# ScalarE's Silu of the z gates issued one projection step earlier in a Mamba-2 scan

## The reference

```python
zxbcdt = h @ w_in
z, xbc, dt = jnp.split(zxbcdt, ...)
xbc = jax.nn.silu(causal_depthwise_conv(xbc, conv_w, conv_b))
...                      # xs, bmat, cmat from xbc
y = ssd_chunked_scan(xs, dt, a, bmat, cmat) + d_skip * xs
y = rms_norm(y * jax.nn.silu(z), norm_w)
return y @ w_out
```

## Time and profile before

| | |
|---|---|
| median of 3 runs | 1496.96 us (1496.11 to 1497.39) |
| the profiled execution, its own time | 1497.73 us |
| its span | 1495.9 us |
| granted TensorE clock, mean | 0.991 |
| TensorE (matmul) busy | 1437.1 us, 96% |
| weight loads busy | 976.6 us, 65% |
| VectorE busy | 995.1 us, 67% |
| ScalarE busy | 747.6 us, 50% |
| DMA | 506.01 MB, mean 338 GB/s |

### The profile page before, as it was taken

One profiled execution on the slowest core, in us unless ns is written; L12 is line 12 of the kernel. 1 busy time (PEld: TensorE's weight loads), 2 busy tenths in 40 slices (PEclk: granted clock), 3 DMA queues, 4 the chain that ended last, 5 costly groups with the idle time before them and its releaser, 6 DMA issues.

```text
span 1495.9 us, 18527 instructions
## 1 busy us (share of the span) xinstructions
PE 1437.1 (96%) x6840; PEld 976.6 (65%) x6840; DVE 995.1 (67%) x1271; ACT 747.6 (50%) x977; POOL 18.6 (1%) x27
## 2 busy tenths in 40 slices
PE   7989999999999899999999999999999989999998
PEld 2835787888789778674666556756465655565573
DVE  2578788888659899764666646765654555655563
ACT  3565544444455896353446445644453444545361
POOL 0000000000000000000100000000000000000000
PEclk9999999999999999999999999999999999999999
DMA  9878698888366545679999999999999999999996
GB/s 361 330 248 292 240 396 303 301 295 301 103 217 185 162 161 204 261 288 409 364 412 406 411 374 416 418 420 420 409 420 413 420 420 418 413 420 414 420 419 247
DMA packets 118201, 506.01 MB, mean 338 GB/s; under 512 B 13779, under 2 KB 16492, under 8 KB 83032
## 3 DMA queue, kind: packets, MB, share of 16 engines
q1 hardware_dynamic: 115640, 496.51, 85.6%
q0 software_dynamic: 2464, 8.24, 1.6%
HBM read 502.52 MB, written 2.32 MB: 337 GB/s over the span
## 4 chain that ended last, share of the span: by engine, by line
PE 74%; DVE 10%; DMA 7%; ACT 6%; issue 3%; SPq 0%; DVEq 0%; ACTq 0%
PE acc L2685 16%; PE acc L2693 16%; PE acc L2686 16%; PE acc L3187 15%; DVE w_lo L1581 3%; ACT w_hi L1038 2%; DVE cv L2308 2%; DMA raw_rest<-in_moe_w_down 1%; DMA raw<-in_moe_w_down 1%; PE xb L3071 1%; DMA mod<-in_moe_w_gu 1%; PE acc L2834 1%; DMA mod<-in_moe_w_down 1%; DMA raw<-in_ada_w 1%; ACT dec L1487 1%
## 5 line engine op out<-in xcount | busy, mean ns | idle before, releaser
L1581 DVE TENSOR_TENSOR w_lo<-raw,w_hi 128x1024 fp32r<-128x1024 f32 x356 | 427.3, 1221 | 136.6 <-ACT w_hi L1038 126.1
L1038 ACT ACTIVATE w_hi<-raw 128x1024 fp32r<-128x1024 f32 x356 | 371.0, 1057 | 249.1 <-PE acc L2693 157.7
L2685 PE MATMUL acc<-w_hi,g_hi 128*128 128x512 f32 x448 | 179.3, 400 | 4.0 <-ACT w_hi L1038 3.9
L2686 PE MATMUL acc<-w_hi,g_lo 128*128 128x512 f32 x448 | 174.8, 390 | 0.0
L2685 PE MATMUL acc<-w_hi,a_hi 128*128 128x512 f32 x384 | 155.4, 405 | 8.5 <-ACT z_s L1404 7.7
L2686 PE MATMUL acc<-w_hi,a_lo 128*128 128x512 f32 x384 | 151.4, 394 | 0.0
L2693 PE MATMUL acc<-w_lo,g_hi 128*128 128x512 f32 x448 | 139.1, 392 | 4.1 <-DVE w_lo L1581 4.1
L3187 PE MATMUL acc<-raw,g_s 128*64 128x512 f32 x592 | 131.6, 594 | 0.5 <-DMA raw<-in_moe_w_gu 0.5
L2693 PE MATMUL acc<-w_lo,a_hi 128*128 128x512 f32 x384 | 119.5, 392 | 0.0
L1581 DVE TENSOR_TENSOR w_lo<-mod,w_hi 128x1024 fp32r<-128x1024 f32 x66 | 78.5, 1221 | 60.0 <-ACT w_hi L1038 58.2
L2685 PEld LDWEIGHTS acc<-w_hi,g_hi 128*128 128x128 f32 x448 | 84.2, 188 | 38.4 <-issue 12.7
(11 more groups left out here) (417 smaller groups left out, 2057.3 us busy)
## 6 DMA issues: line engine op xcount, KB each, us to landing
raw<-in_moe_w_gu SPq DMA_DIRECT2D x136, 1024.0 KB, 14.8
raw<-in_moe_w_down SPq DMA_DIRECT2D x66, 1024.0 KB, 16.5
raw<-in_ada_w SPq DMA_DIRECT2D x96, 512.0 KB, 6.0
mod<-in_moe_w_gu SPq DMA_DIRECT2D x40, 1024.0 KB, 13.8
raw<-in_ffn_w_gu SPq DMA_DIRECT2D x56, 512.0 KB, 5.9
mod<-in_moe_w_down SPq DMA_DIRECT2D x23, 1024.0 KB, 16.3
raw_more<-in_moe_w_gu SPq DMA_DIRECT2D x22, 1024.0 KB, 14.3
raw<-in_ssm_w_in SPq DMA_DIRECT2D x40, 512.0 KB, 5.0
```

The costliest lines, as they stand in the source:

```text
L1038: act.activation(w_hi[:, w % SPLIT, :], raw_tile(no), ACT.Copy).then_inc(hi_ready, 1)
L1581: dve.tensor_tensor(w_lo[:, w % SPLIT, :], raw_tile(no), r32(w_hi[:, w % SPLIT, :]), ALU.subtract).then_inc(raw_used, 1)
L2685: pe.matmul(o, l_hi[:, k, rows_], hi[:, col:col + HALF], start=new, stop=False)
L2686: pe.matmul(o, l_lo[:, k, rows_], hi[:, col:col + HALF], start=False, stop=False)
```

## The change

`z_of_group(j)` is issued at ScalarE's step `PROJ_END[Z0 + j] + 1` (28, 32, 36, 40) and no longer at `+ 2` (29, 33, 37, 41), and within the step it stands behind the first place of `conv_silu` and ahead of `unit_decays`. No instruction of the program text is added or removed, and no other engine's list is touched.

```diff
                 if i not in DECAYS_FIRST:
                     conv_silu(i)
+                for j in range(SG):
+                    if i == PROJ_END[Z0 + j] + 1:
+                        z_of_group(j)
                 for u in range(NU):
                     if i == unit_in_at(u) + LEAD:
                         unit_decays(u)
                 if i in DECAYS_FIRST:
                     conv_silu(i)
-                for j in range(SG):
-                    if i == PROJ_END[Z0 + j] + 2:
-                        z_of_group(j)
                 for u in range(NU):
                     if i == PROJ_END[Z0 + u // 2] + 4 + u % 2:
                         y_square(u)
```

## The result

The changed kernel takes 1500.18 us (median of 16 runs, 1498.16 to 1503.26) beside 1496.12 us (16 runs, 1493.79 to 1497.39). The ratio is 1.003, 95% interval 1.0022 to 1.0037: 4.5 us slower (3.3 to 5.5) by the ratio; the two medians lie 4.06 us apart. The forecast was 1500.2 us, against a median before of 1496.96, which is 3.2 us slower.

What follows compares the result with a forecast made beforehand. VectorE and ScalarE were taken to bound steps 28 to 39, so VectorE's lateness of 0.97, 3.06, then 5.32 us made step 40 2.65 to 3.75 us late; 3.2 taken, 1496.96 + 3.2 = 1500.2 us, range 1495.2 to 1502.5.

Steps and rivals of the forecast that it cites:

- The number: Whole kernel: 3.2 us slower, 1500.2 us against the median of 1496.96.
- What bounds the stage: Steps 28 to 39: VectorE and ScalarE, feeding each other, set the pace; TensorE runs behind them, so its gains shorten nothing.
- Step 28: z now lies ahead of the Exp VectorE awaits: VectorE 0.97 us late; TensorE's 6.0 us wait goes but its lead is returned.
- Step 32: Two table loads more ahead of `w_hi` of step 33: it is 4.64 us late, VectorE 3.06 us late.
- TensorE's pause: Before step 33, waiting for a transposed block's copy: TensorE stands still for 4.7 us and the clock falls to the low level.
- The price of a load: ScalarE's table load: 1.28 us by its row, adding 1.3 to 1.4 us; a rival at twice that gave 1505, chance 0.04.
- Step 36: z and two loads ahead of the Exp: Exp 6.73 us late, VectorE's product 4.96 us late, `w_lo` of step 37 5.32 us.
- the signs: Marks of being right: VectorE waits some 2 us for `w_hi` of step 33 and 1.9 us for step 36's Exp, among others.
- Step 40: TensorE's start, after z and the turned y: +2.65 us, or 3.75 with a longer low clock; 3.2 taken.
- the length of the low clock after step 32: TensorE at half speed after its pause: 3.2 us gives 2.65 us at step 40, a whole 5.02 us tile 3.75.
- To the end: Behind step 40: TensorE keeps the delay and adds none; the router and SyncE's expert loads come that much later, all let through.
- The clock falling at step 40: Rival: TensorE waits about 1.5 us there and the clock falls, 1.7 to 2.3 us more, 1501.3 to 1503.0; chance 0.23.

Runs made afterwards that it cites:

- group 0: Kernel before with only the z Silu of step 29 moved, to step 28 behind the convolution's Silu; ratio 0.9995.
- group 2: Kernel before with only the z Silu of step 37 moved, to step 36 ahead of the decays; ratio 0.9996.
- two loads alone: Kernel before with one 128 x 1 Silu into a spare tile added ahead of step 32's decays, nothing moved; ratio 1.0007.
- group 1 alone: Kernel before with only the z Silu of step 33 moved, to step 32 ahead of the decays; ratio 1.0037.
- the change without group 1: Changed kernel with one z Silu left at step 33, the other three moved as in the change; ratio 1.0019 against the kernel before.
- the last but one run: Kernel before with z Silus moved to steps 28, 32 (behind the convolution's Silu) and 36 (behind the decays), step 28's decays put first; ratio 1.0001.
- group 2 behind the decays: Kernel before with only the z Silu of step 37 moved, to step 36 behind the decays and ahead of `w_hi` of step 37; ratio 0.9997.

## Why the prediction was right, point by point

- **The number**: the sum of +3.2 us stands a little under what was measured, 3.88 us in the stage and 3.3 to 5.5 us in the timing. That 1500.2 meets the median of 1500.18 so closely is luck: the median before came out 0.84 us lower than the one the forecast was added to, and the slowdown larger by about as much.
- **What bounds the stage**: right for the change. Taking away TensorE's waits for z gained 0.57 us (group 0) and nothing (group 2), and the same stage of 64.06 us came out with 3.95 and with 1.91 us of wait before step 32. It isn't the whole truth of the kernel before: there the turned y was done at 570.19 and TensorE came to step 40 only at 573.00, some 2.7 us later than the 0.1 us behind y that the change needs (575.77 to 575.88), so TensorE with its low clock set that moment. The turned y has 2.7 us to spare there, and its 6.58 us of lateness (575.08 - 569.50 + 1.00) make the 3.88.
- **Step 28**: VectorE late by 0.97 us, measured 0.97.
- **Step 32**: `w_hi` of step 33 late by 4.64, measured 4.63; VectorE late by 3.06, measured 3.04; its wait 2, measured 1.98. TensorE's pause 4.7, measured 4.47, and the clock fell in it. The price of a load is its row (two loads alone: 1.17 us of wait for 1.3). The Trainium skill (ScalarE: Activation LUTs, section What ACT_TABLE_LOAD costs) adds about 1.4 us for each change of table; no row here shows it.
- **Step 36**: 4.96 without the second z Silu waiting for TensorE, 1.1 more with it. It waited, 1.12 us in both halves, and VectorE is 6.16 us late; its wait for the Exp is 3.15 us where the signs had 1.9.
- **Step 40**: +2.65 to +3.75 was forecast, 3.2 taken, 3.88 measured. The mis-sized term is the length of the low clock after step 32: it lasted from 538.29 to about 543.4, 5.1 us, the long end of 3.2 to 5.4. With the long end the sum gives 3.75, so the step that was too small is the low clock's length by way of the wait for z, and what is left is 0.13 us.
- **To the end**: the delay reached the loads of the experts whole (75.49 and 75.47 us from step 40), SyncE's wait before them was 15.0 us as in the earlier trace rows.
- **The clock falling at step 40** didn't come in the change (wait of 1.10 us where 1.5 was forecast, clock 1.00) and did in one experiment, where it made the way from step 40 to the load 1.6 us longer (77.08 for 75.48); the forecast had 1.7 to 2.3.

What the forecast had missed showed only in experiments: a z Silu moved forward can wait for TensorE's tile, and with it all that stands behind it in ScalarE's list (group 1 alone, the change without group 1). In the change itself this was 1.12 us and stood in the sum.

## What to carry to other kernels

Before an instruction is moved forward to end the longest wait in the list, find out which engine sets the pace of the stage: if the waiting engine isn't it, the wait comes back at the next thing that the busy engines make, as it did here. Count what the new place does to the tables of ScalarE and to whatever stood behind it, one step at a time; the same Silu cost 1.8 us less on the far side of an Exp that another engine waits for. When two engines hand work back and forth, an experiment that keeps or undoes one part alone can be as slow as the whole change or nearly (group 1 alone, the change without group 1), so undo parts in more than one combination.

## What the runs showed of the hardware

- The length of a pause of TensorE doesn't tell whether the granted clock falls. It fell after 1.73 us (before, step 36) and stayed up over 2.42 us (the change, step 29). The same pause in the same place went both ways: 1.91 us before step 31 (fell with group 0 alone, stayed up in the change) and 1.03 us before step 40 (fell in the last but one run, stayed up with group 2 behind the decays). In those two falls TensorE was already at work again. From its next matmul or from the fall on, the clock stayed low for some 3 to 6 us.
- Executions of the same instructions came to the mark at 504.05 to 508.99 us. That spread, of 5 us, arises ahead of the steps in question and is as large as the largest effect here, so distances from a mark in the trace told in one execution what five rounds of timing could hardly tell. They are no stand-in for the timing: VectorE's part of the stage repeats closely (its product for the unit of step 36, line 2368 and up to 3 lines lower, at 44.42 to 44.45 us from the mark in four executions), but the low clock doesn't (3.3 and 6.2 us at step 36).
- A table load took 1.28 us in all of these runs, and can run while the Silu behind it still waits: in the run with group 1 alone it was over 2.73 us before its Silu began.
